# A deeper pipeline and another split of engines in the q/k/v/g preparation of a hybrid encoder

## The reference

```python
def _rope(x, cos, sin):
    x1, x2 = x[..., :half], x[..., half:]
    return jnp.concatenate([x1 * cos - x2 * sin, x2 * cos + x1 * sin], axis=-1)

# _diff_branch: 2048 tokens, q, k, v, g of 512 columns each
    q, k, v, g = jnp.split(u, 4, axis=-1)
    q = _rope(_rmsnorm(q, qk_norm_w[0]), cos, sin) * (d ** -0.5)
    k = _rope(_rmsnorm(k, qk_norm_w[1]), cos, sin)
    ...
    return o.reshape(b, L, DIFF_WIDTH) * jax.nn.silu(g)

# _na_branch
    qg = to_grid(_rmsnorm(q.reshape(b, L, h, d), qk_norm_w[0]) * (d ** -0.5))
    kg = to_grid(_rmsnorm(k.reshape(b, L, h, d), qk_norm_w[1]))
```

## Time and profile before

| | us |
|---|---|
| median of 2 runs | 4368.66 (4357.32 and 4380.01) |
| the profiled execution | 4356.85 |
| its span on the slowest core (core 7) | 4355.3 |
| spans of the other cores | 4331.3 to 4354.0 |
| mean granted TensorE clock, all cores | 0.742 to 0.746 |

### The profile page before, as it was taken

The page is one execution under the profiler, slowest core; times in us unless marked ns, Lnnn a source line. Parts: engine busy times, 40 slices in busy tenths (PEclk is TensorE's granted clock), DMA queues, the critical chain, the costliest instruction groups (busy, mean ns, idle before and its releaser), DMA issues.

```text
span 4355.3 us, 54863 instructions; the slowest of 8 cores (4331.3 to 4355.3 us)
## 1 busy us (share of the span) xinstructions
PE 2461.6 (57%) x16848; PEld 1306.8 (30%) x16848; DVE 1860.6 (43%) x3555; ACT 1961.8 (45%) x2885; POOL 715.2 (16%) x656
## 2 busy tenths in 40 slices
PE   1665556675557347443654656555856583464439
PEld 1223333333444114111222223333334351232214
DVE  1453332365622663563113532333656316635641
ACT  3235556444423564463111346564444334654640
POOL 0120000000001551552001210000000005524530
PEclk9887888795558568666887877887965586686669
DMA  5002000004111342244322020000031113422345
GB/s 124 12 1 42 6 5 6 5 1 90 52 34 26 103 120 36 85 120 134 116 67 38 1 41 6 6 5 6 1 77 52 46 18 98 115 52 81 111 129 184
DMA packets 185128, 244.91 MB, mean 56 GB/s; under 512 B 70268, under 2 KB 150140, under 8 KB 182792
## 3 DMA queue, kind: packets, MB, share of 16 engines
q1 hardware_dynamic: 132776, 205.60, 15.1%
q0 software_dynamic: 52064, 35.79, 6.1%
HBM read 226.27 MB, written 50.86 MB: 64 GB/s over the span
## 4 chain that ended last, share of the span: by engine, by line
PE 29%; ACT 23%; DVE 18%; issue 17%; DMA 7%; POOL 4%; DVEq 1%; ACTq 1%; SPq 0%; POOLq 0%
PE psall L233 19%; ACT arena L209 19%; DVE arena L213 9%; PE psall L232 8%; POOL arena L213 4%; ACT L209 4%; DVE arena L227 3%; DVE arena L223 2%; DMA arena<-na_tab 2%; DVE arena L245 2%; PE psall L237 2%; DVE arena L249 2%; DMA arena<-x 1%; DMA arena<-w_in 1%; DVE arena L218 1%
## 5 line engine op out<-in xcount | busy, mean ns | idle before, releaser
L233 PE MATMUL psall<-arena 128*128 128x512 bf16 (+3 forms) x8280 | 1838.0, 387 | 1052.0 <-ACT arena L209 558.9
L209 ACT ACTIVATE arena<-arena 128x8 f32<-128x8 f32 (+9 forms) x1232 | 740.3, 606 | 1420.6 <-DVE arena L213 635.1
L233 PEld LDWEIGHTS psall<-arena 128*128 128x128 bf16 (+1 forms) x8280 | 739.4, 112 | 1923.7 <-issue 1480.8
L209 ACT ACTIVATE arena<-psall 128x1024 bf16<-128x1024 f32 (+6 forms) x1196 | 941.8, 808 | 737.2 <-PE psall L233 454.1
L213 DVE TENSOR_TENSOR arena<-arena 128x512 f32<-128x512 f32 (+7 forms) x1192 | 905.2, 760 | 695.2 <-ACT arena L209 396.9
L232 PE MATMUL psall<-arena 128*128 128x129 bf16 (+4 forms) x7232 | 583.9, 235 | 421.8 <-ACT arena L209 352.8
L213 POOL TENSOR_TENSOR arena<-arena 128x512 bf16<-128x512 f32 (+2 forms) x568 | 660.9, 1175 | 865.5 <-DVE arena L213 803.2
L232 PEld LDWEIGHTS psall<-arena 128*128 128x128 bf16 (+1 forms) x7232 | 470.4, 111 | 632.4 <-issue 628.5
L213 DVE TENSOR_TENSOR arena<-psall,arena 128x512 f32<-128x512 f32 (+1 forms) x466 | 264.1, 578 | 705.3 <-PE psall L233 316.0
L227 DVE COPY arena<-psall 128x512 bf16<-128x512 bf16 (+3 forms) x386 | 199.5, 542 | 510.8 <-PE psall L232 438.3
L237 PE MATMUL psall<-arena 128*128 128x128 bf16 (+1 forms) x1336 | 148.8, 261 | 415.6 <-DVE arena L223 190.3
(11 more groups left out here) (8 smaller groups left out, 69.2 us busy)
## 6 DMA issues: line engine op xcount, KB each, us to landing
arena<-csT_d SPq DMA_DIRECT2D x64, 1024.0 KB, 6.1
arena<-x SPq DMA_DIRECT2D x48, 512.0 KB, 5.2
arena<-na_tab SPq DMA_DIRECT2D x16, 1344.0 KB, 6.2
arena<-w_in POOLq DMA_DIRECT2D x20, 1024.0 KB, 9.8
yT<-arena SPq DMA_DIRECT2D x128, 128.0 KB, 1.9
arena<-yT SPq DMA_DIRECT2D x8, 2048.0 KB, 15.1
arena<-w_out POOLq DMA_DIRECT2D x8, 1024.0 KB, 25.6
sf_d<-arena SPq DMA_DIRECT2D x64, 128.0 KB, 1.7
```

What stands on the lines that cost most here:

```text
L209: return lambda e: e.activation(out=out, in_=in_, func=func, **kw)
L233: return lambda e: e.matmul(out, lhsT, rhs, start=start, stop=stop)
```

## The change

It touches `prep_qkvg` alone.

- With RoPE there are three buffers in place of two for `raw`, `ss8`, `tbuf`, `ubuf` and `rbuf`, and the transposes lag two tiles behind (`LAG = NB - 1`). Without RoPE both stay at 2 and 1.
- `chain` is cut in three. `chain_a` is Square and the sum per head, `chain_b` Ln and Exp, `chain_c` the rest. A tile now issues a for q and k, b for q and k, c for q and k, in both branches.
- With RoPE the two sine products of q go to VectorE; those of k stay on GpSimd.
- With RoPE the raw copies of q and k go from VectorE to ScalarE.

```diff
-    NB = 2
+    NB = 3 if rope else 2
+    LAG = NB - 1
...
-    def chain(tt, i):
+    def chain_a(tt, i):
+        b = tt % NB
+        P.op("act", ACT(sq[i], raw[i][b], AF.Square), reads=[t_raw[i][b]], writes=[t_sq[i]])
+        P.op("dve", RED(ss8[i][b], sq[i].rearrange("p (g d) -> p g d", d=64)), reads=[t_sq[i]], writes=[t_ss8[i][b]])
+
+    def chain_b(tt, i):
+        b = tt % NB
+        s8, t_s8 = ss8[i][b], t_ss8[i][b]
+        P.op("act", ACT(s8, s8, AF.Ln, scale=1.0 / 64, bias=c.epsc), reads=[t_s8, c.t_eps], writes=[t_s8])
+        P.op("act", ACT(s8, s8, AF.Exp, scale=-0.5), reads=[t_s8], writes=[t_s8])
+
+    def chain_c(tt, i):
...
+            eng_u = "pool" if i == 1 else "dve"
-            P.op("pool", TT(u3[:, :, 0:32], t3[:, :, 32:64], bc(TS_[:, tt, 0:32].unsqueeze(1), [128, 8, 32]), ALU.mult),
+            P.op(eng_u, TT(u3[:, :, 0:32], t3[:, :, 32:64], bc(TS_[:, tt, 0:32].unsqueeze(1), [128, 8, 32]), ALU.mult),
...
-    for tt in range(NT + 1):
+    for tt in range(NT + LAG):
...
-                P.op("dve", CP(raw[i][b], ps[banks[i]]), reads=[tps[banks[i]]], writes=[t_raw[i][b]])
+                if rope:
+                    P.op("act", ACT(raw[i][b], ps[banks[i]], AF.Copy), reads=[tps[banks[i]]], writes=[t_raw[i][b]])
+                else:
+                    P.op("dve", CP(raw[i][b], ps[banks[i]]), reads=[tps[banks[i]]], writes=[t_raw[i][b]])
...
-            for i in range(2):
-                chain(tt, i)
+            for stage in (chain_a, chain_b, chain_c):
+                for i in range(2):
+                    stage(tt, i)
...
-        if tt >= 1:
-            transposes(tt - 1)
+        if tt >= LAG:
+            transposes(tt - LAG)
```

More of the change, by code:

```diff
@@ L533, in chain @@
         tb_, t_tb_ = tbuf[i][b], t_tb[i][b]
[L534 to L537, removed]
         t3 = tb_.rearrange("p (g d) -> p g d", d=64)
@@ L545, in chain @@
             u3 = ub.rearrange("p (g d) -> p g d", d=64)
-            P.op("pool", TT(u3[:, :, 0:32], t3[:, :, 32:64], bc(TS_[:, tt, 0:32].unsqueeze(1), [128, 8, 32]), ALU.mult),
+            eng_u = "pool" if i == 1 else "dve"
+            P.op(eng_u, TT(u3[:, :, 0:32], t3[:, :, 32:64], bc(TS_[:, tt, 0:32].unsqueeze(1), [128, 8, 32]), ALU.mult),
                  reads=[t_tb_, t_tab], writes=[t_ub_])
-            P.op("pool", TT(u3[:, :, 32:64], t3[:, :, 0:32], bc(TS_[:, tt, 32:64].unsqueeze(1), [128, 8, 32]), ALU.mult),
+            P.op(eng_u, TT(u3[:, :, 32:64], t3[:, :, 0:32], bc(TS_[:, tt, 32:64].unsqueeze(1), [128, 8, 32]), ALU.mult),
                  reads=[t_tb_, t_tab], writes=[t_ub_])
```

## The result

The kernel became faster. The ratio of its time to that of the kernel before is 0.952, with a 95% interval of 0.947 to 0.956. The profiled execution took 4160.88 us (span 4159.3) against 4356.85 before: 196 less, where 189 were forecast (4168).

The account below looks back on a forecast made before the run. VectorE's serial order was taken to pace RoPE; in NA, E tiles waited on a TensorE bank freed by a Silu. 4356.9 - 114 (RoPE) - 76 (NA) = 4167, say 4168 us; range 4142 to 4235.

Parts of the forecast that it names:

- Which stages, and that they are independent: Whole kernel: only the four prep_qkvg stages gain, RoPE 114 us and NA 76 us in all; nothing else moves.
- Order: All four stages: the second reduce and round trip leave VectorE's path, saving 1.48 us for each tile.
- the rule: RoPE: VectorE's serial pieces summed give the pair of tiles, 27.7 us against 28.03 measured before the change.
- Raw copies: RoPE: moving two raw copies to ScalarE takes 1.50 us a tile off VectorE's path.
- ScalarE's room: RoPE: ScalarE's two added copies, taken at 0.6 us, fit its slack, 2.2 in O tiles, 3.6 in E.
- Sine products: RoPE: q's two on VectorE, 0.42 us each, spaced 0.34, make 2.53 into 1.67, saving 0.86 a tile.
- The lateness that I added: RoPE E tiles: slow TensorE matmuls after a restart make the reduce late; taken as 0.3 us a pair.
- The total for RoPE: Each RoPE stage: 8 x (7.7 - 0.3) - 2.2 = 57 us saved; twice, 114.
- Third buffer and lag 2: RoPE: TensorE starts a whole VectorE tile ahead; one more closing round costs 2.2 us a stage.
- NA: NA stages: pair falls from 20.54 to 15.5 us, the third bank after 1.3 idle; 37.8 saved a stage.
- The rule of the Trainium skill weighed there: NA: dense matmuls on three cores of a die lower the clock to 13/16; pair 18.5, kernel about 4213 us.
- rival 1: NA: TensorE slower because its clock drops; kernel 4183 to 4190 us, or about 4213; chance 0.13 in all.

Follow-up runs that it names:

- e2: Kernel before with the new order in the NA stages alone, RoPE issuing as before: core 7 span 4274.1 us, total 4303.3 on core 2.
- e1: Kernel before with only the new order, in all four stages: core 7 span 4221.0 us, profiled execution 4261.1 on its slowest core, core 2.
- e4: Changed kernel with the raw copies of q and k on VectorE again in RoPE: 4207.7 us profiled.
- e5: Changed kernel with q's sine products on GpSimd again in RoPE: 4179.7 us.
- e10: e9 with the two half-width sine products of a chain tracked as two tiles: 4112.6 us profiled, ratio to the kernel before 0.937.
- e3: Changed kernel with two buffers and lag 1 in RoPE again: 4160.8 us, against 4160.9.
- e6: Changed kernel with k's multiply by the norm issued right behind q's, ahead of q's sine and cosine products, in RoPE: 4117.9 us.
- e9: e7 with k's sine products on VectorE too, so GpSimd does nothing in the RoPE stage: 4110.2 us.
- e7: e6 with RoPE's transposes and their copies issued between Exp and the multiplies: 4095.1 us profiled, ratio to the kernel before 0.943.

## Why the prediction was right, point by point

*Which stages, and that they are independent.* Right (e2, and the sum of the four differences).

*Order.* The terms held. RoPE: 1.48 a tile, 16 tiles, 23.7; e1 showed 25.9 and 25.2. What is above 23.7 is mostly the reduce's late start in four E tiles of the kernel before, which the rule didn't have: it was read from one pair, and that pair was without it. In NA order is the whole gain.

*Raw copies.* Forecast at 1.50 a tile, 24 in a stage; e4 showed 1.5 a tile and 22.8 in a stage (mean of the cores), since the first tile doesn't count. The cover that was named, ScalarE's room, held: the 128x512 f32 copies took 0.60 there and delayed no reduce.

*Sine products.* Their own duration, interpolated to 0.42, was 0.425. Their spacing was mis-sized. I let the second overlap the first (0.34), as neighbours in the trace do. But both write one tracked tile, so the planner sets a wait between them, and the spacing is 0.53. The term is 1.86, not 1.67, and moving them saves 0.67 a tile, not 0.86; e5 showed 10.8 / 16 = 0.67, and e10 got the 0.19 back for each chain by tracking the halves apart. The kernel and the planner's rule, both told ahead of the prediction, were enough to see it.

*The lateness that I added* (0.3 a pair, the reduce waiting for Square after a slow restart) never came: in the changed kernel the reduces of the stage wait for ScalarE only once, at its start. Two errors of one size and opposite effect on the working, 0.38 missing and 0.3 too much, met in a pair of 20.3. The total for RoPE, 57, against 58.7 and 57.4 (57.7 and 57.4 in the mean of the cores), was right partly by that luck, and partly because the late reduces of the kernel before, some 2 us a stage that were gained, made up for the first tile's raw copies, which gained nothing.

*Third buffer and lag 2.* That they only cost was in the working, but I said of them that TensorE starts a whole VectorE tile ahead, as if they gave that. e3 shows the same start with two buffers. Their price was put at 2.2 and is 1.3 to 1.5, since I forgot the copies that the second tile no longer makes.

*NA.* Forecast 37.8 a stage, measured 40.2 and 39.5 on core 7, 38.6 and 39.3 in the mean of the cores. VectorE's and TensorE's chains, each counted at 15.0, mesh at 15.17 and not at the 15.5 that I took. The idle ahead of the third bank is 0.30, not 1.3, because the transposes come later than I had them: 2.04 behind the first copy (848.93 - 846.89) and not 1.10, straight behind the matmuls of the tile before, on which TensorE was still busy.

*Rivals.* The clock did not fall under the dense load in the profiled execution: it was granted at 1.00 in the NA row above, with TensorE busy for 49.1 of 50 us, and the other seven cores had 1.00 and 48.5 to 49.1 us in the same stretch. The rule of the Trainium skill weighed there (13/16 with three busy cores of a die) did not hold there. But the level that it names does occur in another run, and it costs what the prediction feared. In e1 cores 0 and 1 had this in the NA stage of the first layer, here core 0:

```profile
850.00:900.00 50.00, 50.00 (x228) 22.55 (x227) 33.09 (x56) 26.08 (x54) 0.00 (x0) 0.81 0.00 0
```

The granted clock is 0.81, which is 13/16, TensorE is busy all the time, and a pair takes 17.9 instead of 15.2 (18.5 was the estimate). The stage took 146.9 and 144.6 on these two cores, and 129.4 to 130.2 on the other six, which had 1.00 from 850 to 900 us. So rival 1 was real, near the price given for it, and nothing in the working said that the profiled execution would be free of it: that was luck. What brings the level on is not shown. RoPE was fed in time although part of its matmuls ran at the lower level.

*Where the gain stands.* For the first RoPE stage from the first reduce on, mean of the eight cores: 222.8 before, 197.3 in e1, 187.8 in e4, 175.8 in e5, 163.5 in e3 and 164.9 after. Order is worth 25.5 (before less e1), the raw copies 22.9 (e4 less after), the sine products 10.8 (e5 less after). They add up to 59.2, and the third buffer takes 1.5 back: 57.7, where 57.8 was measured.

## What to carry to other kernels

Where in-order engines hand work to each other in a chain, list the start-to-start spacings of the pacing engine, and cost a change by what it takes out of that list: here it gave the order and the raw copies to within 2 us in 25, and missed in the sine products one wait that the dependency tracking puts in. Issue independent steps of two chains side by side before buying depth; the order was worth 25 us a RoPE stage and 39 an NA stage, the third buffer minus one and a half. And look at who is idle in the new order, too: k's multiply, moved ahead of q's products, gave 22 to 23 us a stage more.

## What the runs showed of the hardware

VectorE and GpSimd slow each other when both work on float32 tensors in SBUF. Beside GpSimd's products a 128x512 product with two inputs took 1.04 instead of 0.69 us and a 128x256 one 0.77 instead of 0.43; GpSimd's mean went from 722 to 770 ns (e6), and all of VectorE's loss was gone without GpSimd (e9). Two sine products take 2 x 0.53 = 1.06 of VectorE's time in its own queue; given to GpSimd they saved only 6.20 - 5.82 = 0.38 (e9 against e7), since 0.7 came back as slower work beside GpSimd.

The Trainium skill (SBUF — State Buffer, SBUF: two separate sides) says that the two share a port pair and that an instruction holds it whole while the other blocks. That VectorE instructions with two SBUF inputs suffer agrees. The size agrees in part: a VectorE product that started within one of GpSimd's (193.55 within 193.26 to 194.03, and 194.42 within 194.18 to 194.90) would by a full block start its work only at the end of that one, 0.48 later, 0.96 for the two; the rows show 0.34 each. Whether the rest is the profiler's view of GpSimd's ends or a weaker block is not shown. VectorE's first sine product (193.03 to 193.45) had its usual length, since it was at work first; GpSimd's, which began beside it, took 0.77 instead of 0.72.

TensorE's granted clock can differ between cores that run the same dense stage in the same execution: 0.81 on cores 0 and 1 and 1.00 on the other six in e1, from 850 to 900 us of each core's span, which made a stage bound by TensorE 15 to 17 us longer.
